# Three edits to VectorE's and GpSimd's work in the attention rounds, and the stick-breaking stage without its 38 extra products

## The reference

```python
# first block, selected and windowed attention; second block, attention in chunks with a bias
prob = softmax(q k^T * scale + mask or bias);  o = prob v        # first block: times a gate per head

# second block, stick-breaking attention
z = q k^T * scale
log_fail = where(before, log_sigmoid(-z), 0)
later = cumsum(log_fail, reverse) - log_fail
a = where(before, exp(log_sigmoid(z) + later), 0)
o = a v
```

## Times and the profile before

| | us |
|---|---|
| three runs | 1627.51, 1629.06, 1633.07 |
| median | 1629.06 |
| the profiled execution, its own time | 1627.64 |
| its span, first to last instruction | 1625.9 |
| PE busy | 1528.8 (94%) |
| DVE, ACT, POOL busy | 843.5, 671.9, 191.1 |
| granted clock of TensorE, mean | 0.97 |

### The profile page before, as it was taken

How to read it: one execution, slowest core, us unless ns; L and a number is a source line. 1 busy time by engine, 2 the same in 40 slices (tenths; PEclk the granted TensorE clock), 3 DMA queues, 4 the chain that set the end, 5 groups by cost and what they waited for, 6 DMA issues and landing times.

```text
span 1625.9 us, 22121 instructions
## 1 busy us (share of the span) xinstructions
PE 1528.8 (94%) x8610; PEld 1274.9 (78%) x8610; DVE 843.5 (52%) x1448; ACT 671.9 (41%) x1295; POOL 191.1 (12%) x276
## 2 busy tenths in 40 slices
PE   4999999799989999999999999987989999999997
PEld 2768877577988888888888886666988888888986
DVE  5774645577365444432275436765555444432364
ACT  4323246367543232231353218966442323222453
POOL 0000000143130000000130002364310000000111
PEclk9999999799999999999999999988999999999998
DMA  9523250000403333333403331001123333333321
GB/s 373 195 77 92 92 193 10 0 2 4 153 19 106 96 95 98 93 101 93 141 14 104 93 102 65 1 1 50 55 66 90 101 92 100 94 110 95 120 78 52
DMA packets 40387, 143.06 MB, mean 88 GB/s; under 512 B 4448, under 2 KB 6512, under 8 KB 39792
## 3 DMA queue, kind: packets, MB, share of 16 engines
q1 hardware_dynamic: 38240, 129.55, 25.4%
q0 software_dynamic: 1488, 11.52, 1.8%
q10 hardware_dynamic: 576, 0.85, 0.1%
HBM read 139.81 MB, written 2.10 MB: 87 GB/s over the span
## 4 chain that ended last, share of the span: by engine, by line
PE 79%; DVE 9%; ACT 6%; issue 3%; DMA 1%; POOL 1%; SPq 0%; DVEq 0%; ACTq 0%; POOLq 0%
PE B L276 23%; PE B L277 23%; PE B L278 23%; PE B L1567 2%; ACT T L525 2%; PE B L1808 2%; PE B L1649 1%; DVE WADA L1014 1%; DVE WL L968 1%; PE B L1444 1%; PE B L1546 1%; POOL T L461 1%; DVE X L979 1%; ACT WH L525 1%; DMA X<-in_x 1%
## 5 line engine op out<-in xcount | busy, mean ns | idle before, releaser
L276 PE MATMUL B<-UH,WH 128*128 128x512 f32 (+1 forms) x1120 | 425.6, 380 | 14.5 <-DVE UL L1023 5.8
L277 PE MATMUL B<-UL,WH 128*128 128x512 f32 (+1 forms) x1120 | 418.4, 374 | 0.0
L278 PE MATMUL B<-UH,WL 128*128 128x512 f32 (+1 forms) x1120 | 418.1, 373 | 0.0
L276 PEld LDWEIGHTS B<-UH,WH 128*128 128x128 f32 x1120 | 213.6, 191 | 56.4 <-DVE UL L986 7.7
L277 PEld LDWEIGHTS B<-UL,WH 128*128 128x128 f32 x1120 | 213.7, 191 | 38.2 <-issue 1.9
L278 PEld LDWEIGHTS B<-UH,WL 128*128 128x128 f32 x1120 | 213.5, 191 | 36.7
L525 ACT ACTIVATE WH<-RAW 128x1024 fp32r<-128x1024 f32 x178 | 186.1, 1049 | 121.7 <-DMA RAW<-in_stream 117.9
L968 DVE TENSOR_TENSOR WL<-RAW,WH 128x1024 fp32r<-128x1024 f32 x98 | 121.8, 1246 | 168.9 <-ACT WH L525 168.9
L1264 DVE TENSOR_TENSOR WL<-RAW,WH 128x1024 fp32r<-128x1024 f32 x80 | 98.0, 1226 | 76.7 <-ACT WH L525 73.9
L525 ACT ACTIVATE T<-B 128x256 f32<-128x256 f32 (+4 forms) x165 | 71.2, 434 | 157.9 <-PE B L278 85.7
L525 ACT ACTIVATE T<-T 128x512 f32<-128x512 f32 (+3 forms) x131 | 68.6, 525 | 126.4 <-DVE T L1268 119.2
(11 more groups left out here) (338 smaller groups left out, 3006.1 us busy)
## 6 DMA issues: line engine op xcount, KB each, us to landing
RAW<-in_stream SPq DMA_DIRECT2D x202, 512.0 KB, 3.6
WADA<-in_w_ada SPq DMA_DIRECT2D x4, 2048.0 KB, 19.1
RAW<-in_stream SPq DMA_DIRECT2D x16, 384.0 KB, 3.4
WADA<-in_w_ada SPq DMA_DIRECT2D x4, 1024.0 KB, 18.4
W<-in_w POOLq DMA_DIRECT2D x2, 2048.0 KB, 12.1
X<-in_x SPq DMA_DIRECT2D x2, 1024.0 KB, 10.2
DECAY<-in_decay POOLq DMA_DIRECT2D x1, 2048.0 KB, 8.1
X<-in_x POOLq DMA_DIRECT2D x2, 1024.0 KB, 8.0
```

The lines of the kernel that those rows point to most:

```text
L276: nc.tensor.matmul(out, lh, rh, start=start, stop=False, **kw)
L277: nc.tensor.matmul(out, lh, rl, start=False, stop=False, **kw)
L278: return nc.tensor.matmul(out, ll, rh, start=False, stop=stop, **kw)
```

## The change

Four edits.

1. In BAND GpSimd's multiplication by the reciprocal gets a second factor, a column of ones (`CONST[:, 2, 0:1]`), where it had one factor alone.
2. In the softmax rounds, NSA and BAND, VectorE's reciprocals of pair m-1 move from the head of round m to its end.
3. In the stick-breaking rounds VectorE's max of unit n-1 goes ahead of its subtraction for unit n-2.
4. The 38 products of line 1444 in the stick-breaking stage go. Those of the first projections and ahead of NSA (line 1444 too) stay.

```diff
                     if x["gate"] is None:
-                        ins = nc.gpsimd.tensor_scalar(w, w, rec, None, ALU.mult)
+                        ins = nc.gpsimd.tensor_scalar(w, w, rec, CONST[:, 2, 0:1], ALU.mult, ALU.mult)
                     else:
                         ins = nc.gpsimd.tensor_scalar(w, w, rec, x["gate"], ALU.mult, ALU.mult)
...
                     ahead(m)
-                    if 1 <= m < N + 1:
-                        for s in range(2):
-                            u = 2 * (m - 1) + s
-                            wait(dve, tag["exp"], u + 1)
-                            tag["rec"].mark(v.reciprocal(RECS[:, u % 8:u % 8 + 1], SUMS[:, u % 8:u % 8 + 1]))
                     if m < N:
...
                             tag["lo"].mark(tt(AL2[:, u % 4, 0:(i + 1) * P], PT_BANK[s][:, 0:(i + 1) * P],
                                               AH2[:, u % 4, 0:(i + 1) * P], ALU.subtract))
+                    if 1 <= m < N + 1:
+                        for s in range(2):
+                            u = 2 * (m - 1) + s
+                            wait(dve, tag["exp"], u + 1)
+                            tag["rec"].mark(v.reciprocal(RECS[:, u % 8:u % 8 + 1], SUMS[:, u % 8:u % 8 + 1]))
...
                     E["sb_m"].mark(ts(Z_RING[n % 4][:, 0:L], B[2 + n % 6][:, 0:L], 40.0, None, ALU.min))
+                if 1 <= n < 33:
+                    u = n - 1
+                    L = P * (u % 4 + 1)
+                    wait(dve, E["sb_l"], u + 1)
+                    wait(dve, E["sb_spl"], u - 3)
+                    E["sb_sp"].mark(tt(SP_RING[u % 4][:, 0:L], B[2 + u % 6][:, 0:L], Z_RING[u % 4][:, 0:L], ALU.max))
                 if 2 <= n < 34:
                     u = n - 2
...
                     E["sb_spl"].mark(tt(SPL[:, o:o + L], SP_RING[u % 4][:, 0:L], SPH[:, o:o + L], ALU.subtract))
-                if 1 <= n < 33:
...
             for n in range(32 + 7):
                 if n == 2:
-                    keep_clock(8, QAH[:, 0, :], B[1])
                     wait(pe, E["p5_vlo"], 8)
...
                     wait(pe, E["sb_p"], n - 5)
-                    if n >= 2:
-                        keep_clock(1, VAH[:, 0, :], B[2 + n % 6])
```

## The result

The changed kernel takes 1637.87 us (median of 20 runs, 1629.07 to 1646.94); the kernel before, beside it, 1628.6 (20 runs, 1621.24 to 1633.07). The ratio is 1.0063, with a 95% interval of 1.0048 to 1.0077: slower by 9.3 us, more than the 0.3% that can be told from no change. The forecast was 1623.5, with a range of 1619 to 1628 and one for 8 in 10 that ended at 1633; the case that came true is the rival in which the clock swings. The profiled execution took 1636.37 us (span 1634.5), with a mean granted clock of 0.959, where before had 0.970.

What follows compares the result with a forecast made beforehand. PE bounds the stick-breaking stage, with ACT next; in BAND nothing is full. Stick-breaking -4.8 + 3.2 = -1.6, BAND -3.4, NSA 0: -5.0 us, so 1623.5 us for the median; range 1619 to 1628, 8 in 10 from 1617 to 1633.

Steps and rivals of the forecast that it cites:

- the rival in which the clock swings: Steady stick-breaking stage: short units drop the clock in every head, 3.2 us a fall; five falls more, 1637 us; chance 0.13.
- the clock's term of the sum: Stick-breaking stage: without the products TensorE falls to 1.2 GHz once more in the steady part, costing 3.2 us.
- The price of a microsecond at the low level: Stick-breaking stage: PE runs at half pace during a 6.8 us fall, so one in the steady part costs 3.2 us.
- The case that I built on it: Stick-breaking stage: the clock holds, no fall after the start; -9 us with a little at NSA's end, 1619.5 us; chance 0.27.
- ACT as the next bound, 8.75 us a head: Stick-breaking stage: without products ACT sets the pace, a head takes 8.75 us instead of 9.41, 3.8 us less over 5.8 heads.
- over 97%: Sign for the forecast in the stick-breaking stage: ACT over 97% busy, PE waiting, heads at 8.6 to 9.0 us.
- The loop around VectorE's max: Stick-breaking rounds: SPL, max, mask, SPH loop takes some 8 us per four rounds; max first opens it, tail 1.0 us less.
- The 8 products at the start: Stick-breaking start: they take 2.10 us, but PE then waits for VectorE's VBL anyway, so removing them gains 0.
- The second factor: BAND: GpSimd's scaling of 512 columns falls from 1564 to 773 ns; at most 1.1 us a group goes.
- The later reciprocals in NSA: NSA: PE is full there, so the waits on VectorE cost nothing; 0, between -1.5 and +1.5 us.
- BAND: BAND stage: -3.0 us over three groups, -0.4 at the end; -3.4 in all, between -7 and +1.
- the BAND rival: BAND gives nothing: later reciprocals delay GpSimd's start as much as it is faster; 1627.5 us, no change; chance 0.22.

Runs made afterwards that it cites:

- the kernel with products at the start only: Changed kernel with the 8 products back and two single ones in each of rounds 2 to 7, none later: 1627.72 us, ratio 1.0011.
- the best one: Edits 1 to 3, the 8 products, two single ones in each of rounds 2 to 7, then one per short round: 1618.35 us, ratio 0.9942.
- all products back: Changed kernel with the 38 products of the stick-breaking stage put back, edits 1 to 3 kept: 1624.00 us, ratio 0.9975.
- 64 rows: Edits 1 to 3 with the 30 single products on 64 rows instead of 128, the 8 as before: 1631.81 us, ratio 1.0028.
- the short-rounds kernel: Edits 1 to 3, single products only in short rounds (15 of 30): 1622.46 us, ratio 0.9976, with the 8; 1619.70 us, ratio 0.9965, without.

## Why the prediction was wrong

**The step that failed** is the clock's term of the sum, +3.2 us: "I take one more fall, 3.2 us, as near the number in the stage now." The runs put it at some +14. The trace of the changed kernel has 58 us at the low level in the stage where before had 7.4. It is not a freak of one execution: over 20 runs the low time is 146 us on average (121 to 178), 47 more than before. The argument's direction was right (what goes is denser than what stays, the short units are the thinnest part). Its number was not: it took from one profile both how long a fall lasts (6.8 us) and how many to expect (one). In the profiles with the same products at the start (edits 1, 2 or 3 alone, or all three) the stage has 24 to 31 us at the low level, most of it in one stretch, with a first head of 14.3 us; yet their low time per run (88 to 103 us) is about that of before (99). So where the low stretches lie and how long they last differs between kernels, and perhaps executions, that differ in nothing said here, and the 7.4 us of one trace was no number to scale from. The rival's five falls of 6.8 us (34 us) were nearer to the 47, and too few still.

**The price of a microsecond at the low level** was also off, the other way: 3.2 / 6.8 = 0.47 forecast. Over the changed kernel's 20 runs a line of time against low time rises by 0.30 us a us; the kernel with products at the start only gives 0.31, the best one 0.27. In others, whose low time varies less, it is anything from 0.11 (all products back) to 0.42 (64 rows). One head wholly low takes 12.40 us (988.06 to 1000.46) against 8.8 where the clock holds, so (12.4 - 8.8) / 12.4 = 0.29. I had charged the low level with half of PE's pace throughout; a head needs 8.1 us of PE by my own sum, and 12.4 is 1.5 times that, not twice. With both sizes mended the sum comes out: 47 x 0.30 = +14.1, edits 1 to 3 -4.9, together +9.2; measured +9.3. That 0.30 is a fit over runs, not a separate experiment, and the agreement to 0.1 us is luck: the interval of the -4.9 alone, 0.9965 to 0.9985, is 3.3 us wide, and the sum counts nothing for the time that the missing products set free.

**The Trainium skill's rule** ("TensorE: Matmul & The Clock Gate", section "Why this matters for your kernels") would have the clock hold as long as PE has no long pauses. The trace disagrees more clearly than before: PE was busy for 51.94 of 55 us, none of its waits from 983 to 1070 was over 1.2 us, and the clock fell again and again. (The prediction's "longest pause" of 0.62 us held with the 8 products only; without them it is 2.65 us, once, at the start.) The case that I built on it (0.27) was wrong.

**ACT as the next bound, 8.75 us a head: right where the clock holds.** In the changed kernel itself no head ran at 2.4 GHz throughout. But in the kernel with products at the start only, two heads did without any product: 8.57 and 8.89, on average 8.73 us, with ACT on the chain. Its busy share there was 96% (95% with two products a head), not the "over 97%" that was to show it. The split was other than the prediction's, though. It put the 0.66 us a head down to the products that go; of the 9.41 us, 0.36 go with the max ahead of SPL, all products kept (9.05), and at most 0.32 with the products. At most, since the first of the two heads follows a low stretch, in which the other engines may have got ahead of PE; that is argued, and two heads of one trace are all there is.

**The loop around VectorE's max: there, but its size was misread.** With half of the products it takes 9.13 and 9.63 us a head with the loop, 8.8 and 9.03 without, where some 8 us, "just below" PE's 9.41, was said; and it held back the kernel before too, which the prediction put down to PE alone. The time of the kernel moved by 0.7 us, within the intervals.

**The 8 products at the start: right** that they gain nothing, and more: leaving them out in the short-rounds kernel cost nothing either.

**The second factor: right** for the instruction (767 to 774 ns for 773 forecast). **The later reciprocals in NSA: right**, 96.4 us for 96.8. **BAND: partly wrong.** The stage is 2.7 us shorter, near the forecast's 3.4, but not by the way said: three groups were to shrink by 3.0 us and shrank by 0.45. The rest lies ahead of the first exponential of 512 columns: from BAND's first scores to it 9.9 us before (1062.9 to 1072.85) and 7.8 now (1074.0 to 1081.76), with 4.8 and 2.3 us of it at the low level by the clock's records. The sign that I had named for the BAND rival ("BAND's groups stay at 11 us") is there: 33.8 / 3 = 11.3 us, with PE at 22.28 and ACT at 21.18 of 25, none of them full. GpSimd's waits for the reciprocals (10.9 + 6.4 us from 1081 to 1116) are not the price that this rival spoke of: with the second factor alone and the reciprocals in their old place it waits 13.7 + 6.2 us in a stretch as long (1078 to 1113), so they come with the faster scaling. The chain of waits ahead of the second group's exponential runs through VectorE:
```profile
1091.47 0.21 DVE RECS L1208 x2
1091.68 0.65 DVE T L1360
1092.33 0.60 DVE W_S L1194
1092.97 1.52 ACT W_S L525 x4
```
The moved reciprocals now stand behind a round's work, another head's scaling (line 1360) follows, and only then comes the next maximum, for which ScalarE waits. Ahead of the third the chain runs along PE (0.89 us of line 1567 at 1103.30). Which of these holds a group at 11 us no experiment separated.

**Still open.** Why the low stretch at the stage's start lasts 6.8 us in one execution and 24 in another of nearly the same instructions, and how many of the 4.9 us of edits 1 to 3 belong to each. Also open is why the clock holds for 30 us without a product in one kernel and falls again and again in another.

## What to carry to other kernels

A product that nobody reads can be the cheapest thing in a stage: before taking such products out, look at what is left on TensorE between the dense parts, and price the removal by the low time over many runs, not by the stretches of one profile. Where they cost time, halve them rather than drop them: here 15 of 30, in the shortest rounds, did as well as all, and whether more of them where the stage begins add to it was not shown. Compare the mean granted clock as well as the time. When an edit gains on one engine but frees it to wait, ask what the clock does with the waiting.

## What the runs showed of the hardware

- TensorE, once at 1.2 GHz at the stage's start, stayed there for 23.9 us with PE busy for 5.00 of 5 us, doing short products on 64 and 128 rows. From 980 to 1005 it was granted 0.96 and 1.00 in two traces with two products of 128 by 512 in each of the rounds 2 to 7, and 0.53 and 0.86 in two with one a round.
- The clock held at 2.4 GHz for 30 us (1024 to 1054) with PE busy for 25.86 of them and no such product since 990.4, in the kernel with products at the start only; in the changed kernel it fell five times after the first stretch.
- A head wholly at 1.2 GHz took 12.40 us and one at 2.4 GHz 8.8, so a microsecond at the low level cost some 0.3 us here.
- Products on 64 rows did less for the clock than the same on 128: 110 against 96 us at the low level, 1.0028 against 0.9975, on two chips, 7 and 12 runs.
- GpSimd multiplies 128 by 512 fp32 values by one factor in 1564 ns and by two in 767 to 774, so a second factor of ones makes it twice as fast.
- Single scalings took 1737 and 2519 ns, among others of 774 and 1565 in the same kernels. What ran beside them I didn't separate.
